# Issuing the second load of constants from ScalarE behind the first four evictions

## The reference

```python
def rms_norm(x, g):
    xf = x.astype(jnp.float32)
    y = xf * lax.rsqrt(jnp.mean(xf * xf, axis=-1, keepdims=True) + EPS)
    return (y * g.astype(jnp.float32)).astype(x.dtype)

# first_block
x = x + hybrid_mixer(rms_norm(x, norm_mix_g[l]), w_in[l], ...)
# hybrid_mixer
proj = h @ w_in                                  # (512, 1024) @ (1024, 3592)
dq, dk, dv, mq, mk, mv, mo, mi, mf = jnp.split(proj, ...)
# diff_attention
q = rotary(q.transpose(0, 2, 3, 1, 4), pos) * (DA_HEAD_DIM ** -0.5)
k = rotary(k.transpose(0, 2, 3, 1, 4), pos)
```

## Time and profile before

| what | value |
|---|---|
| median of 3 runs | 1760.81 us |
| the 3 runs | 1755.36, 1760.81, 1761.26 us |
| the profiled execution | 1759.36 us |
| its span, first to last instruction | 1757.8 us |
| around the span | 1.6 us |
| PE busy | 1610.4 us, 92% |
| granted TensorE clock, mean | 0.955 |

### The profile page before, as it was taken

The page is one execution under the profiler, slowest core; times in us unless marked ns, Lnnn a source line. Parts: engine busy times, 40 slices in busy tenths (PEclk is TensorE's granted clock), DMA queues, the critical chain, the costliest instruction groups (busy, mean ns, idle before and its releaser), DMA issues.

```text
span 1757.8 us, 15347 instructions
## 1 busy us (share of the span) xinstructions
PE 1610.4 (92%) x5808; PEld 792.1 (45%) x5808; DVE 723.0 (41%) x1529; ACT 478.5 (27%) x980; POOL 363.3 (21%) x348
## 2 busy tenths in 40 slices
PE   7998999999999699988888787899989999999998
PEld 3434456644554333333333333444455554445553
DVE  2856434264242312110110110549775143987612
ACT  2022242101121101100000001566366134735621
POOL 3800000001000111111211110148243012842500
PEclk9998999999999799998898888999999999999999
DMA  9511032457255599999999999602102130020101
GB/s 332 191 49 48 0 120 96 144 191 252 72 214 222 195 401 406 406 406 410 407 404 398 412 414 359 227 1 72 72 1 91 49 113 1 23 98 25 48 0 48
DMA packets 72401, 325.98 MB, mean 185 GB/s; under 512 B 10458, under 2 KB 13682, under 8 KB 59904
## 3 DMA queue, kind: packets, MB, share of 16 engines
q1 hardware_dynamic: 64976, 310.23, 45.3%
q0 software_dynamic: 6144, 10.52, 1.8%
q10 hardware_dynamic: 1200, 4.17, 0.6%
HBM read 320.60 MB, written 12.68 MB: 190 GB/s over the span
## 4 chain that ended last, share of the span: by engine, by line
PE 71%; DMA 21%; DVE 5%; ACT 2%; issue 1%; POOL 0%; SPq 0%; POOLq 0%; DVEq 0%; ACTq 0%
PE bank L190 67%; DMA arena<-in_w 16%; DMA arena<-x_rows,arena 3%; PE bank L2200 1%; DMA arena<-in_w_in 1%; DVE arena L2660 1%; DMA x_rows<-arena 1%; ACT arena L2375 1%; DVE arena L2647 0%; PE bank L680 0%; DVE arena L2662 0%; PE bank L929 0%; PE bank L2147 0%; DMA arena<-y_rows 0%; DMA y_rows<-arena 0%
## 5 line engine op out<-in xcount | busy, mean ns | idle before, releaser
L190 PE MATMUL bank<-arena 128*128 128x512 f32 (+10 forms) x4944 | 1507.8, 547 | 87.5 <-DMA arena<-in_w 51.1
L190 PEld LDWEIGHTS bank<-arena 128*128 128x128 f32 (+5 forms) x4944 | 689.0, 177 | 839.6 <-issue 780.3
L2822 POOL TENSOR_TENSOR arena<-arena 128x512 f32<-128x512 f32 x180 | 198.9, 1105 | 204.4 <-ACT arena L2428 186.7
L1834 DVE SCALAR_TENSOR_TENSOR arena<-arena,bank 64x512 f32<-64x512 f32 x32 | 24.0, 750 | 314.0 <-ACT arena L1247 314.0
L1891 POOL TENSOR_TENSOR arena<-arena 128x1 f32<-128x1 f32 (+2 forms) x44 | 34.2, 777 | 568.1 <-DVE arena L1282 341.3
L2428 ACT ACTIVATE arena<-arena 128x512 f32<-128x512 f32 x180 | 127.0, 725 | 21.1 <-POOL arena L2822 21.1
L1013 ACT COPY arena<-bank 128x512 f32<-128x512 f32 (+3 forms) x115 | 61.2, 539 | 234.1 <-PE bank L190 130.7
L1247 ACT ACTIVATE arena<-bank,arena 64x512 f32<-64x512 f32 x32 | 21.9, 684 | 362.2 <-PE bank L190 362.2
L1912 POOL DMA_INDIRECT y_rows<-arena x32 | 32.4, 1014 | 406.6 <-ACT arena L1258 245.7
L1294 DVE SCALAR_TENSOR_TENSOR arena<-arena 128x512 f32<-128x512 f32 x84 | 78.4, 933 | 2.7
L1827 DVE TENSOR_TENSOR arena<-bank,arena 128x512 f32<-128x512 f32 x32 | 22.1, 692 | 107.5 <-PE bank L929 107.5
(11 more groups left out here) (268 smaller groups left out, 898.1 us busy)
## 6 DMA issues: line engine op xcount, KB each, us to landing
arena<-in_w SPq DMA_DIRECT2D x96, 2048.0 KB, 39.8
arena<-in_w_in SPq DMA_DIRECT2D x15, 2048.0 KB, 9.4
arena<-in_w_ada SPq DMA_DIRECT2D x12, 2048.0 KB, 9.2
arena<-in_w_out SPq DMA_DIRECT2D x6, 2048.0 KB, 7.7
arena<-in_w_xk SPq DMA_DIRECT2D x2, 2048.0 KB, 9.3
arena<-in_w_xv SPq DMA_DIRECT2D x2, 2048.0 KB, 9.2
arena<-in_w_xq SPq DMA_DIRECT2D x2, 2048.0 KB, 9.9
arena<-in_w_xo SPq DMA_DIRECT2D x2, 2048.0 KB, 8.8
```

Of the source, the lines that this page charges most:

```text
L190: i = pe.e.matmul(o, l, r, start=first and j == 0, stop=last and j == len(pairs) - 1)
L2822: pool.e.tensor_tensor(yc, yc, k.prod[l][n % 4], ALU.add).then_inc(*k.pool.step("sum", l, f, j))
```

## The change

ScalarE issues the second load of constants behind the four evictions of `act_features` and no longer ahead of them. The load itself, its target, its semaphore and all waits for it stay as they are.

```diff
     act.wait_ge(*k.c_in.done("params"))
     act.e.activation(k.CACT, k.P("c"), ACT.Silu).then_inc(*A.step("cact"))
+    act_features(k, act, "mix", 4, k.HT, k.P("gmix"))
     act.e.dma_start(k.cst[:, c_first:], a["consts"][:, c_first:]).then_inc(*k.c2_in.step("consts"))
-    act_features(k, act, "mix", 4, k.HT, k.P("gmix"))
     act_mixer_in(k, act)
```

## The result

The changed kernel took 1753.89 us (median of 21 runs, 1750.92 to 1758.71) and the kernel before 1758.05 us (21 runs, 1753.69 to 1761.90). The ratio is 0.9979, 95% interval 0.9971 to 0.9988, so 3.7 us less, between 2.1 and 5.1 (the two medians alone are 4.2 us apart). The forecast was 4.3 us less. The profiled execution of the changed kernel has a span of 1755.0 us.

The account below looks back on a forecast made before the run. The start was taken as bound by the DMA of w_in's block 0, then TensorE. Start 2.47 plus clock 1.84 plus 0 for the moved load made 4.3 us, taking the median 1760.81 to 1756.5; range 1750 to 1764.

Parts of the forecast that it names:

- Part 1: Front DMA: without the 1.05 MB ahead, block 0 of w_in lands 2.6 us earlier, at about 16.5; bounds 0 to 2.6.
- Part 2: PE's projection start: limited by its transposes and first evicted feature, so at about 16.65, not 19.12; gain 2.47 us.
- Part 3: TensorE's clock in the first projection product: the fall to half clock after idling disappears; gain 1.84 us, bounds 0 to 1.84.
- Rival (a): Projection start: the clock falls anyway, so the gain is 2.5 us and the time 1758.3; chance 14%.
- Part 4: Moved load: issued at 16.6, landing at 24.4 (bounds 19.0 to 39.0), tying with GpSimd's first rotary product; cost 0.
- rival (d): GpSimd's rotary product: constants land too late, 5.2 us reach PE, 0.9 us slower than before, 1761.7; chance 6%.
- rival (b): No gain arrives: constants weren't ahead of w_in's last rows, or the gain is lost later; 1760.8; chance 18%.

Follow-up runs that it names:

- e3: Kernel before, with half of the load (cos and sin, 512 KB) at the old place and the rest behind the evictions; profiled span 1751.6 us.
- e6: Changed kernel with the load on SP's queue behind block 0 and ScalarE's two early loads cut to columns the start needs; ratio 0.9970 to the kernel before.
- e2: Changed kernel, with TensorE's qk 0 also waiting for the last evictions and VectorE's lam sums; ratio 1.0014 to the kernel before.
- e10: The kernel of e2 (changed kernel, qk 0 waiting for all features) executed once more under the profiler; span 1755.9 us.
- e4: Changed kernel with the load issued still later, behind ScalarE's copy of qk 1; profiled span 1766.4 us.
- e9: Changed kernel with the load issued later, behind ScalarE's copy of qk 0; profiled span 1756.7 us.
- e1: Kernel before, load at its old place, with three dummy products on TensorE ahead of its wait for block 0 of w_in; ratio 1.0003.

## Why the prediction was right

**Part 1, the bytes.** Block 0 was to land at 16.5. In the first execution it landed at 2.82 + 13.5 = about 16.3 by the DMA view, hidden behind the transposes; in the second PE waited for it until 16.48. The upper bound was the right choice, and e3 fits the linear form that was assumed.

**Part 2, the start.** Forecast 16.65, measured 16.68: 2.44 us of gain and not 2.47. The expected order of waits held in that execution: the end of the transposes, then no catching up with the evictions. In the second the transposes ended at 15.73 and PE stood 0.75 us for block 0, more than the 0.3 us that the prediction allowed. Which of the two limits, near 16.4 and between 15.7 and 16.6, comes last is thus a matter of the execution; they lie so close that the gain of this change ends there, and that the first execution agrees to 0.03 us is partly luck. e6 moved both.

**Part 3, the clock.** The mechanism was right for the kernel before and 1.84 us was too large. The stretches of 200 MATMULs differ by 85.07 - 83.50 = 1.57 us. The step that failed was to set the time from a product's start to its copy (8.72) against the time from copy to copy (6.88): the first of these contains the way from the last MATMUL to the copy. At full clock it is 23.84 - 16.68 = 7.16 us, 0.28 more than 6.88. With it, 2.44 + 1.57 = 4.01, and the stretch ended 4.00 us earlier. The sum had 4.3, and the first copy came at 23.84, just behind the 23.5 to 23.7 that were forecast, for the same 0.28 us. The term is also less firm than it was put: e2 and e10 show 0 and 2.97 us for the same idle time, though the kernel before had a fall every time, 3 of 3. Rival (a) did not come: neither without idle time nor after 0.75 us of it was there a fall.

**Part 4, the load at its new place.** Issue 16.52 (forecast 16.6), landing 24.12 (24.4), GpSimd released by ACT's copy: a tie that cost nothing, as forecast. Reading the early issue at 11.05 ahead of the ACTIVATE at 13.47 as the sequencer running ahead gave the right time. VectorE idles for 7.90 us ahead of L1363, as forecast. What was wrong is the price of rival (d). It took the 7.88 us of VectorE's idle time at 98 us as the cushion, but PE needs VectorE's work already at 69 us, in `pe_mod`. With the cushion of 3.8 us that e4 and e9 show, PE feels a first product of GpSimd that starts later than about 28.4 and not 33.8, and the sign turns near 32.4 and not at 38.1. At the upper bound of 39.0 the change would by this estimate have been 14.4 - 3.8 - 4.0, some 7 us slower than before and not 0.9, beyond the range's upper end of 1764; e4, with 39.63 and a fall of the clock at its stall, ended the stretch 9.1 us later than the kernel before. That case didn't come, so the forecast wasn't hurt, but the range didn't hold it. The Trainium skill (DMA: Bandwidth & Descriptors, Rules for kernel authors) says to issue a DMA early and wait for it late, and the prediction let it speak for this rival. e4 and e9 bear that out from the point on at which the cushion is gone; the changed kernel lies 4 us inside it, and there the early issue was the dearer one, by the 2.64 us that its bytes cost block 0.

**The sum and the rest of the program.** 4.0 us at the end of the stretch, 3.7 us (2.1 to 5.1) in the timed runs: it is carried through within the interval, and rival (b) is not needed. That the whole 4.0 us arrive, both parts of them, is not shown: the part of the clock alone, in e1, left nothing in the total. The median of 1753.89 lies under the 1756.5 of the forecast mostly because the kernel before itself had 1758.05 over 21 runs and not the 1760.81 of the first three.

What follows is noisier than the effect. From the end of the stretch to the chain's store of `x` rows, all in the chain of waits, the three executions of the kernel before took 475.0, 475.1 and 473.4 us, the two of the changed kernel 475.7 and 470.9, e1 472.2 and e6 471.8; the seven others lie between 471.7 and 473.4. From there to the last wait for expert weights it was between 491.4 and 494.7 us in all profiled executions, the most in e6. One execution of the changed kernel has a span of 1755.0 and the other one of 1747.5, with a start alike to 0.2 us. That e1's total shows nothing of its 1.77 us, and e2's is even 0.14% more than before, may be this scatter between groups of 10 to 12 runs, or a real loss in the later stages; the runs don't settle it. That e2 gains nothing over the kernel before is no wonder: its two profiled executions end the stretch at 102.81 and 105.94, on either side of it.

## What to carry to other kernels

Where an engine waits for a load while the DMA engines are full, count the bytes that are moved before it has landed, whoever issued them: at 0.40 MB a us a megabyte not yet needed cost 2.6 us here, and it was as good to put it behind in the same queue as to issue it later from another engine. A load moved back wants its cushion measured along the program order of the engines behind it: the first instruction of the critical engine that needs their work counts, and not the largest idle time. Small columns that the start needs can stand in a load of their own: here that brought the start forward by another 2 us, though the total doesn't show it.

## What the runs showed of the hardware

- With both queues full, each moved as many packets as the other, whatever their size: 80 packets of 8 KB against 81 of 2 KB in 2 us, 83 against 82 after. So the queue with the long rows moved four fifths of the bytes, and the load of constants, issued at 11.05 us, landed (18.85) ahead of block 0 (19.07), which had been issued at 2.82.
- The same idle time of 2.83 to 2.84 us ahead of a product was followed in one execution by no fall of the granted clock, in the other by one that cost 2.97 us. In the kernel before, 2.35, 2.48 and 3.37 us of idle time cost 1.64, 1.57 and 1.73 us. After 3.12 us in e9 and 1.80 us in e3 there was no fall.
